# Moving modulation sums, their folds, one weight load and the mask copies inside a two-block transformer kernel

## The chip, the cores and the metric

The kernel runs on one core of one Trainium2 chip. The metric is the device time of one execution in microseconds (us), as the median of several runs.

## The reference

The input is one sequence of 512 tokens by 1024 channels in fp32, held transposed as 8 tiles of 128 x 512. The first block is the one that the change touches:

```
mod = silu(c) @ ada_w + ada_b             # six vectors of 1024
h = rms_norm(x, g) * (1 + sc_m) + sh_m
proj = h @ w_in                           # 3 mixers and gates
o_a, o_b, o_c = diff_attention, hgrn2 (scan), gla (scan)
merged = g_a*(o_a@w_up_a) + g_b*(o_b@w_up_b) + g_c*(o_c@w_up_c)
x = x + gt_m * (merged @ w_out)           # stage "out"
h = rms_norm(x, g2) * (1 + sc_f) + sh_f
x = x + gt_f * (square(relu(h @ mlp_w1)) @ mlp_w2)
```

The scans of b and c are gated linear recurrences in chunks. A second block follows (windowed attention, two gated convolution networks, a chunked spatial gating unit); the change does not touch it.

## The kernel before

Each fp32 product is made on TensorE in three matmuls: high part by high part, low by high, high by low. A weight unit of up to 128 x 2048 is loaded by SyncE's DMA queue into one of two buffers RAW. ScalarE copies it to WH (L1353) and GpSimd makes WL = RAW - WH (L2659), each in four quarters; `raw_free` is raised when GpSimd has finished, and the queue's next load into that buffer waits for it. SyncE's queue is in order: a load that waits holds back every load behind it.

**Modulation vectors.** The six vectors come from a product of a vector with a matrix. Only a part of it is made at the start. The rest ("shares") is made on VectorE: `shares(j, s)` is four instructions `acc = w * c[k] + acc` (128 x 512, L1917, the very first a plain product at L1914), s = 0 or 1 being the two halves of the 8 slabs. `fold(j)` on TensorE then sums the accumulator over the partitions by four one-column matmuls into a bank of PSUM, and `later_mod(j)` on VectorE adds the bias. Number 4 and 5 give the scale of the second norm, 6 and 7 the gate of the MLP. The matrix for j > 3 arrives by `load_later(a)` (L725) into two buffers LX; it waits until the shares have released the buffer, and sits in the same SyncE queue as the weight loads.

**Stage "out".** TensorE makes 4 tiles of unit ("out", 0), then 4 of ("out", 1), 12 matmuls of 512 columns each, into banks 3, 4, 5, 6 and 0, 1, 2, 3. VectorE empties each tile with one instruction that also adds the residual (X<-PS,MOD,X, L1917). Then `fold(4)` and `tail("out")` follow: units ("out", 2) and ("out", 3) in two halves of 256 columns, 8 output tiles each, with banks 0 to 3 in turn, so that tile k = 4 needs what `take(0, 0)` on VectorE empties. VectorE's order was

```
        shares(4, 0)
        shares(4, 1)
        for j in range(2):
            ... (four evictions of unit ("out", j))
            shares(5, j)
        later_mod(4)
        boundary("out")
```

**Boundary and MLP.** `boundary("out")` takes the tail's tiles, sums squares, scales by the second norm. The MLP is 16 units w1 and 16 units dn. TensorE runs w1 0 to 3, `fold(6)`, w1 4, dn 0, dn 1, `fold(7)`, dn 2, ... . VectorE's `mlp_in(p, i2)` squares and splits what ScalarE's relu left of a w1 unit.

**Scans.** For each of three scans r and 8 levels k a list of steps is placed into the common order of all engines: `product` (TensorE, into banks 4 and 5), `collect` (VectorE copies those banks under a mask into SCT, L2237), `scale` and `differ` for later levels (VectorE, DD, L1911), and after k = 3 `turn` (transposes on TensorE into banks 4 and 5), after k = 4 `state` (48 or 24 small matmuls into bank 4) and `carry` (VectorE, ST). `turn` and `state` need the banks that `collect` empties.

Of the kernel before, what the change touches and what calls it, by code (L numbers as in the profile page):

```python
# [176 lines left out]
class Events:  # L177
# [18 lines left out]
    def at(self, event):  # L196
        if event is None or self.counting:
            return None, 0
        return self.value[event]
# [35 lines left out]
class Plan:  # L235
# [134 lines left out]
    def recurrences(self):  # L370

        yield [("lag", 0)]
        yield [("differ", 0, 0)]
        yield [("expo", 0, 0), ("differ", 0, 1)]
        yield [("scale", 0, 0), ("expo", 0, 1)]
        for g, (r, k) in enumerate(LEVELS):
            for j in range(PAIRS[r]):  # L380
                last = j + 1 == PAIRS[r]
                one, two, three = [("product", r, k, j)], [], []
                if (r, k) == (2, 0):
                    two.append(("read", 1, 0))
                if j == 0 and g + 1 < len(LEVELS):
                    two.append(("scale", *LEVELS[g + 1]))
                if last and g + 2 < len(LEVELS) and LEVELS[g + 2][1] < 7:
                    two.append(("differ", *LEVELS[g + 2]))
                    three.append(("expo", *LEVELS[g + 2]))
                if last and k == 2:  # L390
                    two.append(("ends", r))
                    three.append(("reach_k", r))
                elif last and k == 3:
                    three.append(("turn", r))
                elif last and k == 4:
                    one.append(("eq", r))
                    three.append(("state", r))
                    three.append(("carry", r))
                elif last and k == 5:
                    two.append(("reach_q", r))  # L400
                    if r < 2:
                        three.append(("lag", r + 1))
                elif last and (r, k) == (0, 7):
                    one.append(("read", 0, 0))
                two.insert(0 if last and k in (3, 4) else len(two), ("collect", r, k, j))
                for at_, step in {(1, 0): ((one, 0), (three, 1), (three, 2)), (1, 1): ((one, 3),), (1, 2): ((one, 4), (three, 5), (three, 6)),
                                  (1, 3): ((two, 7),), (2, 0): ((three, 8),), (2, 1): ((three, 9), (three, 10)),
                                  (2, 2): ((two, 11),)}.get((r, k), ()):
                    at_.append(("norm", *(("c", 0), ("c", 1), ("b", 0))[step // 4], step % 4))
                if (r, k) == (1, 1):  # L410
                    three.append(("read", 0, 1))
                yield one
                yield two
                yield three
        yield [("read", 2, 0)]
        for n in range(4):
            yield [("norm", "b", 1, n)]
# [15 lines left out]
def build(nc, wts, xt, vec, mixc, masks, distw, wst, bsr, out, spill):  # L433
# [3 lines left out]
    up, at = ev.up, ev.at  # L437
# [15 lines left out]
    AF = place("AF", o, [8]); o += 32  # L453
# [186 lines left out]
    last_square = {1: 6, 2: 5}  # L640


    FOLDED = [3] * 4 + [7, 4, 7, 7]
    SHARES = [SQ] * 5 + [R, SQ, R]

    def early(*what):
# [8 lines left out]
    def sync_program(q):  # L655
# [73 lines left out]
        while done < len(units) - 9:  # L729
            done += 1  # L730
            load(done)
            for a, (tag, n) in ((10, ("out", 2)), (11, ("out", 3)), (12, ("w1", 0)), (13, ("w1", 0)), (14, ("w1", 3)), (15, ("w1", 4))):
                if done == U[tag, n]:
                    load_later(a)
        for hf in range(2):
# [7 lines left out]
    def tensor_program(q):  # L743
# [108 lines left out]
        def tail(name, u, xs, xk):  # L852

            for hf in range(2):
                four = name == "attn" and hf == 0
                for k in range(4) if four else ():
                    rows_half(BANK["tail", name, k, hf], hf, u[0], 128 * k, range(3), xs, xk, True, False, alone=True)
                for k in range(8):
                    i = u[k // 4]
                    b = BANK["tail", name, k, hf]  # L860
                    if four and k < 4:
                        t = rows_half(b, hf, i, 128 * k, [3], xs[3:], xk[3:], False, True)
                    else:
                        t = rows_half(b, hf, i, 128 * (k % 4), range(4), xs, xk, alone=True)
                    if k % 2:
                        t.then_inc(*up("psum", ("tail", name, k // 2, hf), *([("w", i)] if hf and k % 4 == 3 else [])))
                    elif (name, k, hf) == ("f1", 6, 1):
                        t.then_inc(*up("psum", ("tail_six",)))
                    holds(b, ("y_tail", name, k // 2, hf))
                    if (name, hf, k) == ("out", 0, 5):  # L870
                        fold(5)
                    if hf and k == 1:
                        sums_half(name, 0)

# [229 lines left out]
        def fold(j):  # L1104

            b = FOLDED[j]
            q.wait_ge(*at(("shares", j)))
            free(b)
            for m in range(4):
                t = mm(PS[:, b, m:m + 1], SHARES[j][:, 128 * m:128 * m + 128], ones[:, 0:1], True, True)  # L1110
            t.then_inc(*up("psum", ("folded", j)))
            holds(b, ("later_mod", j))
# [37 lines left out]
        for j in range(2):  # L1150
            tiles(U["out", j], mixed[0:4], [("merged", k) for k in range(4)], 3)
        fold(4)
        tail("out", [U["out", 2], U["out", 3]], mixed[4:8], [("merged", k) for k in range(4, 8)])
        w1 = [P.unit["mlp", "in", 0, n] for n in range(2)]
        head("out", "mlp", w1)
# [751 lines left out]
    def vector_program(q):  # L1907
# [40 lines left out]
        def boundary(n):  # L1948
# [19 lines left out]
            def scale(hf, k):  # L1968
                root = PS[:, ROOT[hf], 0:256]
                q.wait_ge(*at(("root", n, hf)))  # L1970
                if n == "out":
                    if k > 2:
                        q.wait_ge(*at(("h", "mlp", k - 3, hf)))
                    q.wait_ge(*at(("af",)))
                    t = stt(half(T0[1 + k % 3], hf), half(X[:, k, :], hf), gain["mlp"](k), root, MUL, MUL)
                    t.then_inc(*up("d_norm", ("sc", "mlp", k, hf), ("post", n, k, hf)))
                else:
                    if k > 1 or hf:
                        q.wait_ge(*at(("x_post", n, k - 2, hf) if k > 1 else ("x_post", n, 6 + k, 0)))
                    t = stt(half(PS[:, SUMS, :], k % 2), half(Y[:, k, :], hf), post[n](k), root, MUL, MUL)  # L1980
                    t.then_inc(*up("d_norm", ("post", n, k, hf)))
# [38 lines left out]
            for p in range(4):  # L2020
                take(0, p)
                if p > 1:
                    add(0, p - 1)
            if n == "out":
                later_mod(5)
                q.wait_ge(*at(("later_mod", 5)))
                stt(AF[:, :], MOD[:, 32:40], 1.0, v("gmlp", 0, 8), ADD, MUL).then_inc(*up("d_mix", ("af",)))
            add(0, 3)
            take(1, 0)
            if nx is None:  # L2030
# [279 lines left out]
        def later_mod(j):  # L2310
            q.wait_ge(*at(("folded", j)))
            tt(MOD[:, 16 + 4 * j:20 + 4 * j], PS[:, FOLDED[j], 0:4], v("ada_b", 16 + 4 * j, 4), ADD).then_inc(*up("d_ev", ("later_mod", j)))

# [65 lines left out]
        merged_low(7)  # L2379
        shares(4, 0)  # L2380
        shares(4, 1)
        for j in range(2):
            i = U["out", j]
            for m in range(4):
                k = 4 * j + m
                q.wait_ge(*at(("t", i, m)))
                q.wait_ge(*at(("x_again", k)))
                q.wait_ge(*at(("later_mod", 1)))
                stt(X[:, k, :], PS[:, BANK[i, m], :], MOD[:, 16 + k:17 + k], X[:, k, :], MUL, ADD).then_inc(*up("d_ev", ("ev", i, m)))
            shares(5, j)  # L2390
        later_mod(4)
        boundary("out")

        def stage(name, taken, given):
# [7 lines left out]
        def mlp_in(p, i2):  # L2402
            i = U["w1", 4 * p + i2]
            for m in range(2):
                n = 2 * i2 + m
                c = 8 * p + n
                q.wait_ge(*at(("ev", i, m)))
                if c > 1:
                    q.wait_ge(*at(("up_lo", (c - 2) // 8, (c - 2) % 8)))
                a_, b_ = TQ[n % 2][:, :], TQ[2 + n % 2][:, :]  # L2410
                tt(b_, a_, a_, MUL).then_inc(*up("d_mix", ("mlp_sq", c)))
                low(("up_hi", p, n), ("up_lo", p, n), UP[p % 2][:, n, 1, :], b_, UP[p % 2][:, n, 0, :])
            if (p, i2) == (0, 0):
                shares(6, 0)
                shares(6, 1)
            elif (p, i2) in ((0, 3), (1, 0)):
                shares(7, p)

        def mlp_out(p, j):
            i = U["dn", 4 * p + j]  # L2420
# [498 lines left out]
```

## Time and profile before

| | |
|---|---|
| runs shown | 2227.24, 2227.36, 2222.14 us |
| median | 2227.24 us |
| profiled execution, its own time | 2227.24 us |
| its span, first to last instruction | 2224.9 us |
| TensorE busy | 2187.4 us, 98% |
| VectorE, ScalarE, GpSimd busy | 50%, 39%, 48% |
| mean granted TensorE clock | 0.996 of full speed |

The span and the profiled execution's own time differ by 2.3 us, which lie around the span. An engine's busy time is the time in which it had an instruction of its own in work; idle time is listed with the instruction that ended it.

### The profile page before, as it was taken

What the parts mean: (1) busy time and instruction counts of PE and PEld (TensorE: products, weight loads), DVE (VectorE), ACT (ScalarE), POOL (GpSimd) and SP (SyncE); (2) the same over time, 40 slices, a digit from 0 to 9 for tenths busy, and PEclk for the clock granted to TensorE, in tenths of its full rate; (3) what the DMA queues carried; (4) which work ended last, traced back from release to release, by engine and by line L of the source; (5) the groups of instructions that cost most, each with busy time, mean ns of one, the idle gap of its engine ahead of it and who ended that gap; (6) DMA issues with size and microseconds to landing.
All of it is one profiled execution on the core that took longest, in us unless ns stands there. A gap on an engine that the chain in (4) does not pass through costs nothing.

```text
span 2224.9 us, 28773 instructions
## 1 busy us (share of the span) xinstructions
PE 2187.4 (98%) x11670; PEld 1823.6 (82%) x11670; DVE 1103.1 (50%) x1694; ACT 874.5 (39%) x1662; POOL 1068.9 (48%) x812
## 2 busy tenths in 40 slices
PE   7999999999999999999999999999999999999998
PEld 4788777878888888888888888888888889888887
DVE  4774657377622214485862434521634447625253
ACT  4554554353423324475432222543323235323234
POOL 2755554454454446534354454454444454544444
PEclk9999999999999999999999999999999999999999
DMA  7211224574223222212222232232222222222221
GB/s 310 76 60 67 74 86 166 188 290 171 114 97 112 92 98 95 97 58 77 76 95 95 84 109 103 84 114 95 95 95 76 95 95 77 95 100 90 103 105 58
DMA packets 41251, 237.27 MB, mean 107 GB/s; under 512 B 4640, under 2 KB 6816, under 8 KB 15776
## 3 DMA queue, kind: packets, MB, share of 16 engines
q1 hardware_dynamic: 39760, 232.67, 29.3%
q10 hardware_dynamic: 1360, 2.78, 0.4%
q8 instruction: 92, 1.51, 0.3%
q14 instruction: 39, 0.32, 0.0%
HBM read 225.99 MB, written 8.39 MB: 105 GB/s over the span
## 4 chain that ended last, share of the span: by engine, by line
PE 87%; DVE 7%; ACT 2%; issue 1%; DMA 1%; POOL 1%; SPq 0%; DVEq 0%; POOLq 0%; ACTq 0%
PE PS L755 86%; DMA RAW<-in_wts 1%; POOL WL L2659 1%; DVE HLO L1917 1%; PE PS L1202 1%; DVE PS L1917 1%; DVE X L1911 1%; DVE DD L1911 1%; DVE SQ L1917 0%; DVE VV L1914 0%; DVE SCT L2237 0%; DVE R L1917 0%; DVE X L1917 0%; DVE ZB L1911 0%; PE PS L1084 0%
## 5 line engine op out<-in xcount | busy, mean ns | idle before, releaser
L2659 POOL TENSOR_TENSOR WL<-RAW,WH 128x512 fp32r<-128x512 f32 (+1 forms) x688 | 917.8, 1363 | 1015.9 <-ACT WH L1353 990.1
L755 PE MATMUL PS<-HHI,WH 128*128 128x512 f32 x1488 | 594.6, 400 | 1.7 <-DVE HLO L1917 1.2
L755 PE MATMUL PS<-HHI,WL 128*128 128x512 f32 x1488 | 580.6, 390 | 0.0
L755 PE MATMUL PS<-HLO,WH 128*128 128x512 f32 x1488 | 580.4, 390 | 0.0
L1353 ACT ACTIVATE WH<-RAW 128x512 fp32r<-128x512 f32 (+1 forms) x688 | 378.6, 613 | 419.2 <-PE PS L755 380.2
L755 PEld LDWEIGHTS PS<-HHI,WH 128*128 128x128 f32 x1488 | 279.9, 188 | 74.6 <-issue 10.7
L755 PEld LDWEIGHTS PS<-HHI,WL 128*128 128x128 f32 x1488 | 279.8, 188 | 59.6
L755 PEld LDWEIGHTS PS<-HLO,WH 128*128 128x128 f32 x1488 | 280.2, 188 | 57.3 <-issue 2.4
L755 PE MATMUL PS<-UF,WH 128*128 128x512 f32 (+1 forms) x832 | 223.8, 357 | 0.0
L1911 DVE TENSOR_TENSOR T<-PS,R 128x512 f32<-128x512 f32 x112 | 76.9, 690 | 213.9 <-PE PS L755 208.5
L755 PEld LDWEIGHTS PS<-UF,WH 128*128 128x128 f32 x832 | 148.3, 189 | 22.7
L755 PE MATMUL PS<-UP,WH 128*128 128x512 f32 x512 | 157.7, 389 | 0.0
L1911 DVE TENSOR_TENSOR Y<-PS,Y 128x512 f32<-128x512 f32 (+1 forms) x97 | 66.3, 686 | 174.6 <-PE PS L755 174.6
L755 PE MATMUL PS<-UF,WL 128*128 128x512 f32 (+1 forms) x416 | 148.3, 356 | 0.0
L755 PEld LDWEIGHTS PS<-UP,WH 128*128 128x128 f32 x512 | 96.0, 188 | 19.8
L755 PE MATMUL PS<-WH,HHI 128*128 128x256 f32 (+1 forms) x320 | 110.3, 345 | 0.3 <-POOL WL L2659 0.3
L1855 ACT ACTIVATE TG<-TG 128x512 f32<-128x512 f32 x44 | 27.8, 632 | 206.5 <-DVE TG L1917 206.5
L755 PE MATMUL PS<-WH,HLO 128*128 128x256 f32 (+1 forms) x320 | 108.1, 338 | 0.0
L755 PE MATMUL PS<-WL,HHI 128*128 128x256 f32 (+1 forms) x320 | 108.1, 338 | 0.0
L1917 DVE SCALAR_TENSOR_TENSOR TG<-T,V,TG 128x511 f32<-128x511 f32 x88 | 104.5, 1188 | 3.1
L755 PE MATMUL PS<-UP,WL 128*128 128x512 f32 x256 | 99.6, 389 | 0.0
L755 PE MATMUL PS<-US,WH 128*128 128x512 f32 x320 | 99.0, 390 | 0.0
(345 smaller groups left out, 3206.5 us busy)
## 6 DMA issues: line engine op xcount, KB each, us to landing
RAW<-in_wts SPq DMA_DIRECT2D x182, 1024.0 KB, 4.8
LX<-in_wts SPq DMA_DIRECT2D x8, 1024.0 KB, 4.9
FW<-in_wts SPq DMA_DIRECT2D x6, 1024.0 KB, 12.3
spill<-T SPq DMA_DIRECT2D x24, 256.0 KB, 4.0
RAW<-in_wts SPq DMA_DIRECT2D x8, 768.0 KB, 4.1
GT<-spill SPq DMA_DIRECT2D x20, 256.0 KB, 5.1
X<-in_xt SPq DMA_DIRECT2D x2, 1024.0 KB, 6.8
out_x<-X SPq DMA_DIRECT2D x8, 256.0 KB, 2.3
```

The lines of the kernel that those rows point to most:

```text
L755: return e.matmul(o_, l, r, start=start, stop=stop)
L1202: t = e.transpose(PS[:, 2 + part, 128 * s:128 * s + 128], S[:, s, 128 * part:128 * part + 128], ident)
L1353: e.activation(WH[i][:, cs], RAW[i % 2][:, cs], ACT.Copy).then_inc(*up("w_hi", ("w_hi", i, p)))
L1855: e.activation(G, G, ACT.Gelu_apprx_tanh).then_inc(*up("a_ev", ("gelu", name, j)))
L1911: return e.tensor_tensor(o_, a, b, f)
L1917: return e.scalar_tensor_tensor(out=o_, in0=a, scalar=s, in1=b, op0=f1, op1=f2)
L2659: return e.tensor_tensor(o_, a, b, f)
```

## The change

1. In the scans `collect` of level 3 and 4 (the last pair) is no longer put ahead of `scale` and `differ`, but behind them, as for the other levels.
2. `shares(5, 0)` and `shares(5, 1)` are put ahead of the evictions of ("out", 0) and of ("out", 1), instead of behind them; `fold(5)` goes from inside the tail (after tile 5 of the first half) to the place ahead of it, and into bank 6 instead of 4; `later_mod(5)` and the gain AF = (1 + mod) * g go ahead of `boundary("out")`, out of its middle.
3. `shares(6, 1)` goes from behind `mlp_in(0, 0)` to behind `mlp_in(0, 1)`.
4. `load_later(13)` goes from behind the load of ("w1", 0) to behind that of ("w1", 1).

```diff
-                two.insert(0 if last and k in (3, 4) else len(two), ("collect", r, k, j))
+                two.append(("collect", r, k, j))
...
-    FOLDED = [3] * 4 + [7, 4, 7, 7]
+    FOLDED = [3] * 4 + [7, 6, 7, 7]
...
-... (12, ("w1", 0)), (13, ("w1", 0)), ...
+... (12, ("w1", 0)), (13, ("w1", 1)), ...
...
-                    if (name, hf, k) == ("out", 0, 5):
-                        fold(5)
...
         fold(4)
+        fold(5)
         tail("out", [U["out", 2], U["out", 3]], mixed[4:8], [("merged", k) for k in range(4, 8)])
...
-            if n == "out":
-                later_mod(5)
-                q.wait_ge(*at(("later_mod", 5)))
-                stt(AF[:, :], MOD[:, 32:40], 1.0, v("gmlp", 0, 8), ADD, MUL).then_inc(*up("d_mix", ("af",)))
...
         shares(4, 1)
+        shares(5, 0)
         for j in range(2):
             i = U["out", j]
+            if j == 1:
+                shares(5, 1)
             for m in range(4):
...
-            shares(5, j)
         later_mod(4)
+        later_mod(5)
+        q.wait_ge(*at(("later_mod", 5)))
+        stt(AF[:, :], MOD[:, 32:40], 1.0, v("gmlp", 0, 8), ADD, MUL).then_inc(*up("d_mix", ("af",)))
+        q.wait_ge(*at(("af",)))
         boundary("out")
...
-            if (p, i2) == (0, 0):
-                shares(6, 0)
-                shares(6, 1)
-            elif (p, i2) in ((0, 3), (1, 0)):
-                shares(7, p)
+            if (p, i2) in ((0, 0), (0, 1), (0, 3), (1, 0)):
+                shares(6 + (p or i2 == 3), 1 if p else i2 % 3)
```

## Rows read from the trace of the kernel before

**Rows 1.** The page: busy time, share of the span and instructions of each engine.

```profile
PE 2187.4 (98%) x11670; PEld 1823.6 (82%) x11670; DVE 1103.1 (50%) x1694; ACT 874.5 (39%) x1662; POOL 1068.9 (48%) x812
```

**Rows 2.** TensorE's waits: total us, times, longest.

```profile
PE PS L755 <- DVE X L1917: 2.0, 1, 2.0
```

**Rows 3.** Timeline of TensorE, stage "out": start, us, instruction, [idle before it].

```profile
513.55 0.39 PE L755 MATMUL PS<-ME,WL 128*128 128x512 f32 x1
514.45 0.95 PE L755 MATMUL PS<-V,SQ 128*128 128x1 f32 x8
...
523.27 0.50 PE L755 MATMUL PS<-ME,WH 128*128 128x256 f32 x2 [2.01 <-DVE X L1917]
```

**Rows 4.** Window behind that stop: length, busy time of each engine, granted clock, DMA.

```profile
523.00:528.00 5.00, 4.72 (x28) 4.73 (x28) 1.06 (x4) 3.23 (x6) 3.52 (x3) 0.66 0.91 341
```

**Rows 5.** Timeline of VectorE, stage "out" (x: instructions merged into the row).

```profile
508.02 2.71 DVE L1917 SCALAR_TENSOR_TENSOR X<-PS,MOD,X 128x512 f32<-128x512 f32 x4
510.65 0.47 DVE L1914 TENSOR_SCALAR R<-LX,CC 128x512 f32<-128x512 f32 x1
511.16 2.33 DVE L1917 SCALAR_TENSOR_TENSOR R<-LX,CC,R 128x512 f32<-128x512 f32 x3
...
516.04 6.33 DVE L1917 SCALAR_TENSOR_TENSOR R<-LX,CC,R 128x512 f32<-128x512 f32 x4
...
522.36 1.65 DVE L1917 SCALAR_TENSOR_TENSOR X<-PS,MOD,X 128x256 f32<-128x256 f32 x4
```

**Rows 6.** Timeline of GpSimd in the same stage.

```profile
504.54 5.96 POOL L2659 TENSOR_TENSOR WL<-RAW,WH 128x512 fp32r<-128x512 f32 x4 [2.22 <-ACT WH L1353]
515.42 6.39 POOL L2659 TENSOR_TENSOR WL<-RAW,WH 128x512 fp32r<-128x512 f32 x4 [4.91 <-PE PS L755]
```

**Rows 7.** Timeline of SyncE's queue, `load_later(12)` and `load_later(13)`.

```profile
513.52 9.20 SPq L725 DMA_DIRECT2D LX<-in_wts  x2
```

**Rows 8.** Timeline of all engines at the start of the MLP.

```profile
573.24 5.55 DVE L1917 SCALAR_TENSOR_TENSOR SQ<-LX,CC,SQ 128x512 f32<-128x512 f32 x7
575.97 0.43 SPq L665 DMA_DIRECT2D RAW<-in_wts  x1
...
579.19 10.77 SPq L665 DMA_DIRECT2D RAW<-in_wts  x2
582.96 2.20 ACT L1353 ACTIVATE WH<-RAW 128x512 fp32r<-128x512 f32 x4 [10.88 <-DMA RAW<-in_wts]
...
590.71 0.95 PE L755 MATMUL PS<-V,SQ 128*128 128x1 f32 x8
590.85 0.69 DVE L1911 TENSOR_TENSOR UP<-TQ,UP 128x512 fp32r<-128x512 f32 x1 [0.70 <-ACT UP L1758]
```

**Rows 9.** Timeline of all engines, first scan, level 4.

```profile
132.78 1.34 DVE L2237 COPY_PREDICATED SCT<-MASK,PS 128x1024 f32<-128x1024 uint8 x1
134.02 1.80 DVE L1911 TENSOR_TENSOR DD<-Am 128x512 f32<-128x512 f32 x1
134.73 0.88 PE L755 MATMUL PS<-VC,KN 128*32 128x64 f32 x48
135.74 0.28 DVE L2257 COPY ST<-PS 128x128 f32<-128x128 f32 x1
...
137.09 1.19 PE L755 MATMUL PS<-DD 32*128 32x128 f32 x16 [1.48 <-DVE ST L1917]
```

**Rows 10.** Timeline of all engines, third scan, level 3, and TensorE's next wait.

```profile
331.81 1.31 DVE L2237 COPY_PREDICATED SCT<-MASK,PS 128x1024 f32<-128x1024 uint8 x1
333.02 2.12 DVE L1911 TENSOR_TENSOR DD<-QKB,DD 128x512 f32<-128x512 f32 x2
335.06 1.77 DVE L1911 TENSOR_TENSOR DD<-Am 128x512 f32<-128x512 f32 x1
335.75 0.81 PE L1032 MATMUL PS<-V,KH 128*128 128x128 f32 x6
...
347.47 0.50 PE L755 MATMUL PS<-HHI,WH 128*128 128x512 f32 x1 [0.58 <-ACT T L1701]
```

More of the change, by code:

```diff
@@ L731, in sync_program @@
             load(done)
-            for a, (tag, n) in ((10, ("out", 2)), (11, ("out", 3)), (12, ("w1", 0)), (13, ("w1", 0)), (14, ("w1", 3)), (15, ("w1", 4))):
+            for a, (tag, n) in ((10, ("out", 2)), (11, ("out", 3)), (12, ("w1", 0)), (13, ("w1", 1)), (14, ("w1", 3)), (15, ("w1", 4))):
                 if done == U[tag, n]:
@@ L1973, in scale @@
                         q.wait_ge(*at(("h", "mlp", k - 3, hf)))
-                    q.wait_ge(*at(("af",)))
                     t = stt(half(T0[1 + k % 3], hf), half(X[:, k, :], hf), gain["mlp"](k), root, MUL, MUL)
```

## The prediction

> **What bounds the kernel now.** The page comes first: TensorE is busy for 98% of the span, every other engine for at most half of it [rows 1]. So only what stops TensorE, or lowers its clock, costs time, and an edit can win no more than the stops it removes. The list of TensorE's waits comes second: one of 2.0 us on an eviction X of VectorE [rows 2] lies in stage "out", where most of the change lies. Third, the timeline of TensorE there: the fold of shares 4 starts at 514.45, the tail follows, and its tile k = 4 stands still for 2.01 us before 523.27 [rows 3]. Fourth, the granted clock just behind: 0.66 over 5 us [rows 4], a mix of the full 2.4 GHz and of 1.2 GHz. Against full clock that costs 5 x (1 - 0.66) = 1.7 us; below I call this a slow spell. Fifth, VectorE's timeline, which has no gap from 508.02 to the take at 522.36 [rows 5]: the eight shares 5 stand between the evictions and the take that TensorE waits for.
>
> Two prices are read off there. A share costs 2.33 / 3 = 0.78 us when GpSimd is idle and 6.33 / 4 = 1.58 us when GpSimd works [rows 5, 6]; an eviction costs 2.71 / 4 = 0.68 us. Matmuls of 512 columns start every (514.45 - 513.55) / 4 = 0.225 us [rows 3].
>
> **Part 2, stage "out".** The edit removes no work from VectorE; it changes what TensorE meets first.
> - `shares(5, 0)` now starts at 508.02, in place of the first eviction. GpSimd works until 504.54 + 5.96 = 510.50 [rows 6], so two of its four instructions cost 1.58 and two 0.78: it ends at 508.02 + 4.72 = 512.7. The first eviction then ends at 513.4.
> - Who is queued behind: tile 3 of ("out", 1) uses the bank which that eviction frees. It is due 12 matmuls ahead of the fold, at 514.45 - 12 x 0.225 = 511.75. TensorE stops for 1.65 us; ("out", 1) ends at 516.1, `fold(4)` (about 0.9 us) at 517.0.
> - The four evictions end at 512.7 + 2.7 = 515.4. `shares(5, 1)` follows. GpSimd's next pieces start 0.97 us behind the end of ("out", 1) (514.45 to 515.42 [rows 3, 6]), so at 517.1: two shares at 0.78, two at 1.58, end at 520.1.
> - `fold(5)` now stands ahead of the tail and waits for that: TensorE stops from 517.0 to 520.1, 3.1 us. The tail starts behind it.
> - The old stop of 2.01 goes: the take has nothing ahead of it any more. The fold itself is moved, not added. `later_mod(5)` and AF are two tiny instructions and lie beside the tail's first tiles; without that cover they would cost some 0.3 us.
> Stops: 1.65 + 3.1 - 2.01 = +2.7 us. I count one slow spell before and one after. Bounds: all eight shares at 0.78 give 1.25 us of stop and no spell, -0.8 - 1.7 = -2.5; all at 1.58 give stops of 3.3 and 4.75, +6.0, and with a second spell +7.7. I take +2.7, since GpSimd's pieces cover about half of the eight.
>
> **Part 3, `shares(6, 1)`.** Now eight shares 6 run from 572.7 to 578.8 without a gap [rows 8], long ahead of `fold(6)` at 590.71 on TensorE. In the changed kernel the last four wait for `mlp_in(0, 1)`. That step is not early: ScalarE's relu stands behind its conversion of ("w1", 4), which waits for a load issued at 575.97 until 582.96, and VectorE's last instruction of the step ends at about 591.5 [rows 8]. Nothing in the change moves this load: it stands behind `load_later(14)`, which waits for `shares(6, 0)`. Four shares at 0.78 (GpSimd has nothing to do there) end at 591.5 + 3.1 = 594.6. TensorE, in order, stands at `fold(6)` from 590.71 to 594.6: +3.9 us, with ("w1", 4) and all of the rest queued behind. A stop twice as long as the one of rows 3 should bring a slow spell as that one did: +1.7. Sum +5.6. Bounds: 3.9 without a spell; 7.1 with all four at 1.58, 8.8 with a spell.
>
> The Trainium skill ("TensorE: Matmul & The Clock Gate", Part 1: The HAM clock gate) has only these two clocks and ties the low one to idleness and the high one to sustained work. Read strictly, a stop in which `fold(6)` and matmuls stand on both sides need not lower the clock; the sum would then be 1.7 us less. The trace speaks for the spell: 2.01 us of stop were enough [rows 3, 4].
>
> What is late next: `load_later(15)` waits for these shares and holds back the loads behind it, which now go out from 579.19 on [rows 8], to about 595. The first, ("dn", 0), takes some 7 us behind another one (575.97 to 582.96) and lands at 602; its first quarter is ready at about 604. TensorE comes to it at 594.6 + 0.9 + 48 x 0.227 = 606.4. So nothing, with 2 us to spare; if the cover is gone, a stop of 1 to 3 us and perhaps a spell.
>
> **Part 1, `collect` last.** It wins nothing where TensorE does not wait for `scale` or `differ`, and it never does in the list of waits. It costs where TensorE comes to `turn` or `state` early.
> - First scan, level 4: today `collect` 132.78 to 134.02, `differ` 1.80 us beside `state` (134.73, 0.88 us), then `carry` from 135.74, and TensorE goes on at 137.09 [rows 9]. In the new order: `differ` to 134.6, `collect` to 135.8, `state` to 136.7, `carry` 1.35 us to 138.05: +1.0 us. Bounds: 0 (`differ` at an uncontended price) and 1.8.
> - Third scan, level 3: `turn` runs at 335.75 [rows 10]. In the new order `scale` (2.04) and `differ` (1.77) come first, `collect` ends at 331.81 + 3.8 + 1.2 = 336.8: +1.1. At 347.47 TensorE waits 0.58 us for ScalarE, which hangs on a load and not on TensorE; that wait is used up. Net +0.5, bounds 0 and 1.3.
> - At the other places TensorE comes later than all three instructions in either order: 0.
>
> **Part 4, `load_later(13)`.** Today SyncE stands 9.2 us between the two issues [rows 7] and the load of ("w1", 1) behind it; in the new order that load waits for GpSimd's last pieces alone. TensorE waits for neither: 0. If the cover were gone, the later of the two waits would count, 1 to 2 us.
>
> **Sum**, against the profiled execution's own time, 2227.24 (which is also the median): 2227.2 + 1.0 + 0.5 + 2.7 + 5.6 = 2237.0 us.
>
> **Rivals.**
> - A, forecast: stops at tile 3, `fold(5)`, `fold(6)`, and a spell behind the last. 2237, own range 2234.5 to 2240. Chance 0.53.
> - B, the clock stays high behind `fold(6)`, or the first scan and "out" cost only half of what I count: 2227.2 + 1.5 + 2.7 + 3.9 = 2235.3, or down to 2232. For it: the spells are few, 0.996 over the span. Against it: rows 4. Chance 0.22.
> - C, knock-on: ("dn", 0) arrives too late, or "out" has a spell behind each of its two stops. +2 to +4 on A: 2240. For it: 15 us of delay in the weight queue. Against it: 2 us to spare. Chance 0.15.
> - D, not slower: the stop at `fold(6)` does not exist. One mechanism: the conversion of ("w1", 4) gets its load so early that `mlp_in(0, 1)` ends by 590.71 - 3.1 = 587.6, 3.9 us ahead of rows 8; the point is a landing at 579 instead of 583. With the stage "out" at its lower bound the time is 2227.2 + 1.5 - 2.5 = 2226.2. For it: the queue is freed of its 9.2 us stand. Against it: this load is tied to `shares(6, 0)`, not to that stand. Chance 0.10; with it a real gain, which would need nearly all stops of the kernel to go.
>
> **How the numbers follow.** About 0.3% (6.7 us, so 2233.9) is what a measurement of this kernel can tell from no change. Slower by more: nearly all of A and C and a third of B, 0.74. Within: 0.23. Faster: the far end of D, 0.03. The range that should hold 8 in 10 runs from the low part of B to the high part of C: 2231 to 2241.5.
>
> **What would show it.** In TensorE's waits of the changed kernel: one of about 3.9 us at `fold(6)` on a VectorE instruction that writes SQ; one of about 3 us at `fold(5)` on R; one of 1 to 2 us on the first eviction; none on the take; about 2.5 us in all on ST and SCT in the first scan; a low clock behind `fold(6)`. The prediction is wrong if the eight shares 5 end before TensorE has finished ("out", 1), or if `mlp_in(0, 1)` is over long before 591.

## The result, and the profile after

The changed kernel took 2240.73 us (median of 4 runs, 2240.13 to 2245.01), the kernel before 2226.21 us beside it (4 runs, 2222.14 to 2227.36): ratio 1.0073, 95% interval 1.0054 to 1.0091. In a second set of runs it was 2241.94 against 2225.0 us, ratio 1.0077 (1.0062 to 1.0092). The forecast was 2237.0, or +9.8 us; measured are +14.5 and, by the ratios, +16 to +17. The sign held and the sum was too small by some 5 us (by the ratios some 7). The median lies in the stated range, 2231 to 2241.5, but near its upper end: the second set's 2241.94 lies just beyond it, and so does 2243.5, which is the ratio times the 2227.24 that the forecast started from.

The profiled execution has an own time of 2242.2 us. Its line of busy times answers to [rows 1]:

```profile
PE 2192.2 (98%) x11670; PEld 1826.9 (82%) x11670; DVE 1109.5 (50%) x1694; ACT 874.9 (39%) x1662; POOL 1071.9 (48%) x812
```

Nothing shows there: the work is the same, and 15 us are 0.7% of the span. TensorE's waits tell more (us in total, times, longest us):

```profile
PE PS L755 <- DVE SCT L2231: 6.7, 4, 2.5
PE PS L755 <- DVE SQ L1916: 3.8, 1, 3.8
...
PE PS L1030 <- DVE SCT L2231: 2.2, 1, 2.2
PE PS L755 <- DVE R L1916: 2.1, 1, 2.1
PE PS L755 <- DVE X L1916: 1.6, 1, 1.6
PE PS L755 <- DVE ST L1916: 1.4, 1, 1.4
...
PE PS L755 <- DVE T L1910: 1.1, 3, 0.8
```

Against [rows 2], SQ at `fold(6)`, SCT at `turn` (L1030) and R at `fold(5)` are new; the wait on X is now for the first eviction, and the one of 2.0 us on the take is gone. SCT at L755 was 3.2 us in 2 waits before, and is now 6.7 in 4.

The same matmul's start can be compared in the two traces. The difference grows in steps: +1.1 at 134.8 us (`state`, first scan), +4.0 from 336.9 (`turn`, third scan), +3.2 from 348.5 (`state`, third scan), +1.9 over stage "out", +6.7 from 590.3 (`fold(6)`), +1.1 at 1592. That is 18.0; 0.75 is given back at 459. What is left down to 15.5 at the end lies ahead of 142 us and is not of the change: the changed kernel's trace is 2.6 us late by 53 us (1.0 in its first 20 us, 1.6 by low clock), and the other loses 3.0 and 1.5 us to low clock from 107 to 114 and from 138 to 142 us.

The granted clock in the stretches behind those stops (stretch, length, busy times, PEclk, DMA share, GB/s), as in [rows 4]:

```profile
336.00:342.00 6.00, 4.74 (x22) 4.10 (x22) 1.75 (x2) 3.25 (x7) 0.00 (x0) 0.72 0.49 179
353.50:358.50 5.00, 4.21 (x35) 3.64 (x36) 3.27 (x8) 1.26 (x3) 0.65 (x1) 0.70 0.37 102
519.50:525.00 5.50, 3.61 (x20) 3.03 (x19) 5.39 (x7) 2.56 (x5) 1.87 (x2) 1.00 0.69 282
526.00:530.00 4.00, 4.00 (x23) 4.00 (x23) 2.73 (x6) 0.00 (x0) 2.75 (x3) 0.57 0.12 18
601.00:606.00 5.00, 3.66 (x13) 3.28 (x14) 3.57 (x6) 2.21 (x4) 0.00 (x0) 0.52 0.55 175
606.00:610.00 4.00, 4.00 (x15) 3.18 (x14) 2.61 (x5) 1.77 (x4) 0.00 (x0) 0.74 1.01 418
```

Length times (1 - clock) gives what each would cost with TensorE at work throughout: 1.7, 1.5 (1.7 with the 3.5 us that follow, at 0.94), 0, 1.7, and 2.4 + 1.0 = 3.4 us at `fold(6)`. Of the last not all was lost, because the low clock began while TensorE still stood: the fold starts at 602.34, and the window from 601 has the clock at 0.52. The matmuls there fall back by 6.7 us, the stop is 3.8, so 2.9 us were the clock's. In PE's rows a 512-column matmul then takes 0.63 us instead of 0.39.

**Stage "out"** (timeline of all engines; it answers to [rows 3, 5, 6]):

```profile
513.81 1.51 DVE L1913 TENSOR_SCALAR R<-LX,CC 128x512 f32<-128x512 f32 x1
515.36 3.24 DVE L1916 SCALAR_TENSOR_TENSOR R<-LX,CC,R 128x512 f32<-128x512 f32 x3
518.51 2.72 DVE L1916 SCALAR_TENSOR_TENSOR X<-PS,MOD,X 128x512 f32<-128x512 f32 x4
519.31 0.73 PE L755 MATMUL PS<-ME,WH 128*128 128x512 f32 x2 [1.62 <-DVE X L1916]
521.14 3.99 DVE L1916 SCALAR_TENSOR_TENSOR R<-LX,CC,R 128x512 f32<-128x512 f32 x4
523.13 5.61 POOL L2656 TENSOR_TENSOR WL<-RAW,WH 128x512 fp32r<-128x512 f32 x4 [6.66 <-PE PS L755]
525.19 1.05 PE L755 MATMUL PS<-V,R 128*128 128x1 f32 x8 [2.08 <-DVE R L1916]
```

Tile 3 waits 1.62 us for the first eviction, `fold(5)` 2.08 us for the last share. Four shares took 3.99 us, three at 0.75 and one at 1.64 us, the one that began behind the start of GpSimd's pieces at 523.13.

**`fold(6)`** (the same view; it answers to [rows 8]):

```profile
590.67 2.20 ACT L1352 ACTIVATE WH<-RAW 128x512 fp32r<-128x512 f32 x4 [10.89 <-DMA RAW<-in_wts]
...
598.57 0.69 DVE L1910 TENSOR_TENSOR UP<-TQ,UP 128x512 fp32r<-128x512 f32 x1 [0.70 <-ACT UP L1757]
599.18 3.11 DVE L1916 SCALAR_TENSOR_TENSOR SQ<-LX,CC,SQ 128x512 f32<-128x512 f32 x4
602.34 1.87 PE L755 MATMUL PS<-V,SQ 128*128 128x1 f32 x8 [3.77 <-DVE SQ L1916]
```

It is the chain that was forecast: a conversion that waited for its load, relu, the last instruction of `mlp_in(0, 1)`, four shares of 3.11 us, the fold.

**Third scan** (the same view, levels 3 and 4; it answers to [rows 10]):

```profile
329.05 3.17 POOL L2656 TENSOR_TENSOR WL<-RAW,WH 128x512 fp32r<-128x512 f32 x2
331.00 3.21 DVE L1910 TENSOR_TENSOR DD<-QKB,DD 128x512 f32<-128x512 f32 x2
332.18 1.49 POOL L2656 TENSOR_TENSOR DD<-Am 128x512 f32<-128x512 f32 x1
334.14 1.77 DVE L1910 TENSOR_TENSOR DD<-Am 128x512 f32<-128x512 f32 x1
335.83 1.29 DVE L2231 COPY_PREDICATED SCT<-MASK,PS 128x1024 f32<-128x1024 uint8 x1
337.26 0.85 PE L1030 MATMUL PS<-V,KH 128*128 128x128 f32 x6 [2.19 <-DVE SCT L2231]
...
346.32 3.02 POOL L2656 TENSOR_TENSOR WL<-RAW,WH 128x512 fp32r<-128x512 f32 x2 [10.97 <-ACT WH L1352]
348.11 3.22 DVE L1910 TENSOR_TENSOR DD<-QKB,DD 128x512 f32<-128x512 f32 x2
...
352.93 1.30 DVE L2231 COPY_PREDICATED SCT<-MASK,PS 128x1024 f32<-128x1024 uint8 x1
354.29 0.92 PE L755 MATMUL PS<-VB,KN 128*64 128x64 f32 x24 [2.47 <-DVE SCT L2231]
```

GpSimd in the same stretch of the kernel before:

```profile
329.87 3.18 POOL L2659 TENSOR_TENSOR WL<-RAW,WH 128x512 fp32r<-128x512 f32 x2
333.01 1.58 POOL L2659 TENSOR_TENSOR DD<-Am 128x512 f32<-128x512 f32 x1
334.55 1.73 POOL L2659 TENSOR_TENSOR WL<-RAW,WH 128x512 fp32r<-128x512 f32 x1
```

`scale`, the two DD<-QKB, took 3.21 us; before, behind `collect`, it took 2.12 [rows 10]. GpSimd works without a gap in either order, until 336.28 and 335.36. `collect` takes 1.3 us in either place: beside GpSimd it loses nothing. The halves of `scale`, read one by one, take 1.77 and 1.52 us in the new order, 0.67 and 1.53 in the old one. There the first half began at 333.02, within 0.01 us of the start of a new piece of GpSimd; in the new order it began at 331.00, 0.5 us into a piece, and was the longer by 1.1 us. So the same three instructions take 1.1 us longer in the new order, and `turn` is late by 2.2 us and not by 1.1. In each of the seven traces with level 3 of the third scan late the halves take 1.77 and 1.52 us, give or take 0.01; in nine of the ten others they take 0.67 and 1.53.

### The profile page after: what moved, and what is told of

Its sections match the earlier page's. It is cut to its first block and busy times, and to the rows that moved or that the text cites. A ratio compares the mean times of both kernels' runs of the same rounds, so it can differ in the third digit from the quotient of the medians.

```text
span 2240.4 us, 28770 instructions
## 1 busy us (share of the span) xinstructions
PE 2192.2 (98%) x11670; PEld 1826.9 (82%) x11670; DVE 1109.5 (50%) x1694; ACT 874.9 (39%) x1662; POOL 1071.9 (48%) x812
## 5 line engine op out<-in xcount | busy, mean ns | idle before, releaser
L755 PE MATMUL PS<-HHI,WH 128*128 128x512 f32 x1488 | 594.6, 400 | 1.2 <-DVE HLO L1916 1.2
L755 PE MATMUL PS<-HHI,WL 128*128 128x512 f32 x1488 | 581.5, 391 | 0.0
L755 PE MATMUL PS<-HLO,WH 128*128 128x512 f32 x1488 | 581.1, 391 | 0.0
L755 PEld LDWEIGHTS PS<-HHI,WH 128*128 128x128 f32 x1488 | 280.3, 188 | 73.8 <-issue 10.5
L755 PEld LDWEIGHTS PS<-HHI,WL 128*128 128x128 f32 x1488 | 280.2, 188 | 59.3
L755 PEld LDWEIGHTS PS<-HLO,WH 128*128 128x128 f32 x1488 | 280.4, 188 | 57.3 <-issue 2.4
L755 PE MATMUL PS<-UF,WH 128*128 128x512 f32 (+1 forms) x832 | 223.9, 357 | 0.0
L755 PEld LDWEIGHTS PS<-UF,WH 128*128 128x128 f32 x832 | 148.3, 189 | 22.7
L755 PE MATMUL PS<-UP,WH 128*128 128x512 f32 x512 | 157.8, 389 | 0.0
L755 PE MATMUL PS<-UF,WL 128*128 128x512 f32 (+1 forms) x416 | 148.3, 356 | 0.0
L755 PEld LDWEIGHTS PS<-UP,WH 128*128 128x128 f32 x512 | 96.1, 188 | 20.0
L755 PE MATMUL PS<-WH,HHI 128*128 128x256 f32 (+1 forms) x320 | 110.3, 345 | 0.3 <-POOL WL L2656 0.3
L755 PE MATMUL PS<-WH,HLO 128*128 128x256 f32 (+1 forms) x320 | 108.2, 338 | 0.0
L755 PE MATMUL PS<-WL,HHI 128*128 128x256 f32 (+1 forms) x320 | 108.1, 338 | 0.0
L755 PE MATMUL PS<-US,WH 128*128 128x512 f32 x320 | 99.2, 391 | 0.8 <-DVE T L1910 0.8
L755 PE MATMUL PS<-UP,WL 128*128 128x512 f32 x256 | 99.6, 389 | 0.0
```

The source lines that it names most:

```text
L755: return e.matmul(o_, l, r, start=start, stop=stop)
```

## The experiments

Unless said otherwise each is the kernel before with the edit shown. A median is of 5 to 11 executions, and the ratio is to the kernel before, run beside it on the same chip; 0.1% is 2.2 us.

| kernel | median us | ratio | 95% interval |
|---|---|---|---|
| part 1 alone | 2232.67 | 1.0032 | 1.0020 to 1.0044 |
| part 1 alone, again | 2231.56 | 1.0031 | 1.0020 to 1.0043 |
| part 2 alone | 2226.56 | 1.0004 | 0.9995 to 1.0012 |
| part 3 alone | 2231.19 | 1.0027 | 1.0018 to 1.0036 |
| part 4 alone | 2226.28 | 1.0002 | 0.9993 to 1.0011 |
| changed, part 1 undone | 2234.06 | 1.0049 | 1.0034 to 1.0063 |
| changed, part 3 undone | 2235.70 | 1.0050 | 1.0037 to 1.0063 |
| part 1, level 3 only | 2226.61 | 1.0006 | 0.9997 to 1.0014 |
| part 1, level 4 only | 2225.53 | 1.0004 | 0.9995 to 1.0013 |
| part 1, first scan only | 2226.58 | 1.0013 | 1.0003 to 1.0023 |
| part 1, third scan only | 2227.14 | 1.0015 | 1.0003 to 1.0026 |
| `collect` of level 2 first too | 2226.00 | 1.0007 | 0.9998 to 1.0015 |
| shares 5 between the takes | 2220.18 | 0.9979 | 0.9970 to 0.9987 |

### Each part alone

```diff
-                two.insert(0 if last and k in (3, 4) else len(two), ("collect", r, k, j))
+                two.append(("collect", r, k, j))
```

> Part 1 alone: collect of levels 3 and 4 behind scale and differ, all else as before. Theory S (the order of VectorE costs two stops in the third scan, at turn and at state, besides the small one in the first scan): 4 to 8 us slower than before, and the third scan shows one TensorE wait of about 2 us on SCT at turn (L1030 or so) and one of about 2.5 us at state. Theory P (the prediction's: +1.0 in the first scan, +0.5 in the third; the rest of what was seen is the clock's chance): 1 to 2 us slower, with at most one wait of 1 us in the third scan.

Part 2 alone is all of the change's point 2, of which these are the main lines:

```diff
+        shares(5, 0)
         for j in range(2):
+            if j == 1:
+                shares(5, 1)
...
-            shares(5, j)
...
-                    if (name, hf, k) == ("out", 0, 5):
-                        fold(5)
...
+        fold(5)
         tail("out", [U["out", 2], U["out", 3]], mixed[4:8], [("merged", k) for k in range(4, 8)])
...
```

> Part 2 alone: shares 5 ahead of the evictions, fold(5) ahead of the tail. Theory S (two stops of 1.6 and 2.1 us take the place of the one of 2.0): +1.7 us of stops, one slow spell as before, 1 to 3 us slower. Rival (the stage is worth nothing alone, or even wins because the take is no longer late): 0 to 3.7 us faster.

Part 3 alone:

```diff
-            if (p, i2) == (0, 0):
-                shares(6, 0)
-                shares(6, 1)
...
+            if (p, i2) in ((0, 0), (0, 1), (0, 3), (1, 0)):
+                shares(6 + (p or i2 == 3), 1 if p else i2 % 3)
```

> Part 3 alone: shares(6, 1) behind mlp_in(0, 1). Theory S: TensorE stops for 3.8 to 3.9 us at fold(6) and the clock is low for 3.4 to 6.8 us behind it: 5.5 to 7.3 us slower. Rival (the stop is a consequence of the other parts shifting the loads): no stop at fold(6), within 1 us of before.

Part 4 alone:

```diff
-... (13, ("w1", 0)), ...
+... (13, ("w1", 1)), ...
```

> Part 4 alone: load_later(13) one load later. Both theories: within 0.5 us of before; the load of (w1, 1) goes out at 521.8 instead of 522.8. Rival: if the order of the queue matters here, a shift of more than 1 us at the head of the MLP.

**Measured.** By their ratios: part 1 +7.1 us (4.5 to 9.8), part 2 +0.9 (-1.1 to 2.7), part 3 +6.0 (4.0 to 8.0), part 4 +0.4 (-1.6 to 2.4). They sum to 14.4 us, against 16.3 us (12.0 to 20.3) for the whole change. Part 2 alone has its two stops (R 2.1, X 1.6 us) in place of the one of 2.0, as in the changed kernel. Part 3 alone has the stop and one low stretch of the length that was forecast (timeline of TensorE; windows):

```profile
593.00 1.05 PE L755 MATMUL PS<-V,SQ 128*128 128x1 f32 x8 [3.81 <-DVE SQ L1917]
```

```profile
593.00:598.00 5.00, 5.00 (x19) 4.13 (x20) 3.13 (x5) 2.67 (x5) 0.00 (x0) 0.66 0.77 295
```

So 3.8 + 5 x 0.34 = 5.5 us. Part 1 is the surprise. Its waits of TensorE:

```profile
PE PS L755 <- DVE SCT L2237: 4.2, 3, 2.5
...
PE PS L1032 <- DVE SCT L2237: 2.1, 1, 2.1
```

`turn` waits 2.1 us here too, and one SCT wait of 1.0 is new, at `state` of the first scan. The clock behind that `state`, in the kernel before:

```profile
137.00:141.00 4.00, 3.91 (x29) 3.75 (x30) 4.00 (x6) 1.95 (x3) 0.00 (x0) 0.64 0.61 233
141.00:145.00 4.00, 4.00 (x33) 4.00 (x33) 3.15 (x3) 2.12 (x5) 1.40 (x1) 0.94 0.03 6
```

and with part 1 alone:

```profile
137.00:141.00 4.00, 2.80 (x19) 2.58 (x20) 3.93 (x9) 1.99 (x3) 0.00 (x0) 0.65 0.62 242
141.00:145.00 4.00, 4.00 (x21) 4.00 (x20) 3.97 (x4) 0.00 (x0) 0.00 (x0) 0.50 0.00 0
```

1.7 us were lost to the clock there, now 3.4: the stop of 1.1 us is followed by a low stretch twice as long. That is a matter of how often, and not of always: of the seven traces in which level 4 of the first scan is late, five have the long stretch (6.8 us) and the two of the changed kernel have none; of the other ten, three have one of 3.4 us and seven none. On average that is 2.4 us against 0.5, an estimate from 17 traces.

### The changed kernel with one part undone, and part 1 again

> The changed kernel with part 1 undone (collect of levels 3 and 4 first again). If the parts add, as their single runs say (part 1 about 7 us, part 2 about 1, part 3 about 5 to 6, part 4 nothing): 6 to 7 us slower than before, no wait at turn. If part 1 was costly only by itself and not beside the others: 12 to 14 us slower.

> The changed kernel with part 3 undone (shares(6, 1) behind mlp_in(0, 0) again). If the parts add: 7 to 9 us slower than before, and no wait at fold(6). Rival (the stop at fold(6) is due to the late load that part 4 or part 2 moved): the wait stays, 12 us slower or more.

> Part 1 alone once more. Level 3 alone and level 4 alone came out at 1.0006 and 1.0004, both together at 1.0032. Theory S2 (the third scan's stop at turn is 2.1 us in every execution, and what follows depends on whether the clock falls behind it: then TensorE and VectorE are late enough to make a further stop at state): this run gives 3 to 7 us slower again, a turn wait of 2.1 us, and a state wait only if a low clock lies between. Rival (the two levels add to 2 us and the first run was chance): 1 to 3 us slower.

> The kernel before once more, one look: which waits and slow spells come back. Every theory: the same waits (2.5 and 0.8 us on SCT, 1.5 on ST, 2.0 on X) within 0.1 us. Where the clock is low ahead of and behind them may differ; if the spells of the first scan (6.8 and 3.4 us) are missing, they are no property of the kernel.

**Measured.** Without part 1 the change costs 10.9 us, without part 3 11.1 us, whole 16.3: each of the two is worth some 5 us in the company of the others as well, with an uncertainty of some 4 us. Both came out above the 6 to 7 and 7 to 9 us that the single runs had led to expect; the profile without part 1 loses 3.4 us to the clock behind `fold(6)` (0.57 over 593 to 601 us), where part 3 alone lost 1.7. Part 1 alone gave 1.0031 after 1.0032, so its price is no accident of one set of runs. The stops that the change makes come back in every trace to 0.1 us (`turn` 2.1 or 2.2, R 2.0 or 2.1, X 1.6, SQ 3.8 or 3.9). The low stretches do not: the kernel before, profiled a second time (own time 2221.84 us), shows the first line, where its first profile has the second:

```profile
107.00:114.00 7.00, 6.70 (x51) 5.46 (x52) 4.22 (x7) 6.68 (x12) 6.26 (x5) 1.00 0.10 37
```

```profile
107.00:114.00 7.00, 6.38 (x26) 5.25 (x27) 4.43 (x6) 6.51 (x12) 5.93 (x5) 0.53 0.13 56
```

### Part 1 split by level

```diff
-                two.insert(0 if last and k in (3, 4) else len(two), ("collect", r, k, j))
+                two.insert(0 if last and k == 4 else len(two), ("collect", r, k, j))
```

> collect behind scale and differ for level 3 only (level 4 stays ahead of them). If the cost of part 1 lies at turn of the third scan (2.1 us of wait on SCT, often with a slow spell behind it): 2 to 4 us slower than before, that wait present, no wait at the third state and 1.5 us on ST in the first scan as before. If it lies at state: same as before, no wait at turn.

The other half has `k == 3` in that place.

> collect behind scale and differ for level 4 only. If the cost lies at the states: the first scan has a wait of 1.1 us on SCT ahead of state besides 1.4 us on ST, and the third scan's state waits for 1 to 2.5 us: 2 to 4 us slower. If the third state waits only because turn made TensorE and VectorE late before it: no wait there, 1 us slower, all in the first scan.

**Measured.** Level 3 late, expected to cost 2 to 4 us, cost 1.3 (-0.7 to 3.1). It has the wait of 2.2 us at `turn` and no growth of SCT at L755 (3.2 us); level 4 late has SCT 4.2 us and no wait at `turn`. So the stops belong where they were put. The times do not add up as well: 1.0006 and 1.0004 against 1.0032 for both. At the upper ends of their intervals the two would reach 1.0027.

### Part 1 split by scan, and the changed kernel again

```diff
-                two.insert(0 if last and k in (3, 4) else len(two), ("collect", r, k, j))
+                two.insert(0 if last and k in (3, 4) and r > 0 else len(two), ("collect", r, k, j))
```

> The kernel before with collect late (levels 3 and 4) in the first scan only. Theory: ST's and SCT's stops at state of the first scan grow by 1.1 us, no other wait is new, and the low-clock stretch behind them is as long or up to twice as long: 1.1 to 2.8 us slower, ratio 1.0005 to 1.0013. Rival (the unexplained half lies in the first scan, since its stop lengthens the slow spell in every execution): ratio 1.002. The wait of 0.8 us near 1592 us should be absent in both.

The third scan alone has `r < 2` in that place.

> The kernel before with collect late in the third scan only (the second scan stays as before too). Theory: one new wait of 2.2 us at turn, the DVE wait of 0.8 us near 1592 us if it comes from this scan's delay, and a slow spell behind the turn in part of the executions: 2.2 to 4.5 us slower, ratio 1.001 to 1.002. Rival (the halves do not add because the state of the third scan is also late once both levels are late): a wait of 1.5 to 2.5 us on SCT at state near 350 us as well, ratio 1.002 to 1.003.

The changed kernel a second time, 4 executions:

> The changed kernel a second time. The stops (turn 2.2, tile 3 of stage out 1.6, fold(5) 2.1, fold(6) 3.8 us) return with the same lengths to 0.1 us; the low-clock stretches behind them may change place or length; ratio 1.006 to 1.008. Theory: the stop of 2.5 us at state of the third scan is no property of the part alone, since no kernel with part 1 alone shows it; it returns only if the clock falls behind the turn again. Rival: it belongs to the changed kernel and is there whatever the clock does.

**Measured.** Split this way the ratios add, as far as their intervals tell: 1.0013 and 1.0015, 6.2 us of the 7.1. The first scan costs 2.9 us (0.7 to 5.1), the third 3.3 us (0.7 to 5.8). Their profiles show the stops (SCT 4.3 us at L755 in the one, 2.2 us at L1032 in the other). The wait of 0.8 us near 1592 us came in the profile of the first scan's kernel, where it was expected not to.

The changed kernel's second trace agrees with its first to 0.3 us at every matmul, low stretches and the wait of 2.5 us at `state` of the third scan included. Whether that wait needs the low clock behind `turn` can be read beside the kernel with the third scan alone, whose `turn` is just as late but whose clock stays high (timeline of TensorE, windows, timeline of VectorE):

```profile
338.10 0.85 PE L1032 MATMUL PS<-V,KH 128*128 128x128 f32 x6 [2.19 <-DVE SCT L2237]
```

```profile
336.00:341.50 5.50, 3.40 (x22) 3.01 (x24) 2.58 (x3) 3.31 (x7) 0.19 (x1) 1.00 0.32 91
```

```profile
346.58 1.29 DVE L1911 TENSOR_TENSOR DD<-QKB,DD 128x512 f32<-128x512 f32 x2
347.79 1.79 DVE L1911 TENSOR_TENSOR DD<-Am 128x512 f32<-128x512 f32 x1
349.50 1.33 DVE L2237 COPY_PREDICATED SCT<-MASK,PS 128x1024 f32<-128x1024 uint8 x1
```

From the start of `turn`, `scale` starts 8.5 us later here, 10.9 us later in the changed kernel. Here it is nearly done when GpSimd's pieces begin (347.42) and takes 1.29 us; there it meets them and takes 3.22, and `collect` behind it ends too late for `state`. Of the six traces with both levels of the third scan late, the four whose clock stays high behind `turn` lack the second wait, and the two of the changed kernel, with the low clock, have it. That fits the theory (the wait is a follower of the clock), but the clock was not varied by itself, so it is a reading and not a proof.

### Two versions meant to win

First, `collect` of level 2 put first as well, since TensorE waits 2.5 us on an SCT in the kernel before too:

```diff
-                two.insert(0 if last and k in (3, 4) else len(two), ("collect", r, k, j))
+                two.insert(0 if last and k in (2, 3, 4) else len(two), ("collect", r, k, j))
```

> Before, with collect of level 2 put first as well. In the first scan TensorE waits 2.5 us for that collect, which stands behind differ (1.46) and ends (0.16). Theory S: that wait falls to about 1 us: 1 to 3 us faster. Rival: VectorE is the bound of the first scan as a whole and the wait comes back at the next product: within 0.5 us of before.

```profile
PE PS L755 <- DVE SCT L2237: 2.0, 3, 1.0
PE PS L755 <- ACT KN L1632: 1.5, 1, 1.5
```

The wait fell from 2.5 to 1.0 us, and ScalarE, which needs what `differ` writes, is now late by 1.5 us: 1.0007 (0.9998 to 1.0015), nothing won.

Second, the stop of [rows 2] taken away at its root: in the kernel before, `shares(5, 1)` no longer stands as a block ahead of the take, but is cut up between the takes, and `fold(5)` goes behind tile 7:

```diff
-                    if (name, hf, k) == ("out", 0, 5):
+                    if (name, hf, k) == ("out", 0, 7):
...
-            shares(5, j)
+            if j == 0:
+                shares(5, 0)
...
             for p in range(4):
+                if n == "out":
+                    for kk in ((0, 1), (2,), (3,), ())[p]:
+                        ada(5, 1, kk)
                 take(0, p)
```

> Before, with shares(5, 1) cut up between the takes of the tail (two instructions, take 0, one, take 1, one, take 2) and fold(5) behind tile 7 instead of 5. Theory S says the 2.0 us stop at tile 4 of the tail is the take standing behind four shares at 1.6 us; then it goes, with the slow spell behind it: 2 to 3.7 us faster. If the stop were set by the sum of VectorE's work and not by its order, it returns at tile 6 or at the fold: within 1 us of before.

```profile
513.55 2.87 DVE L1917 SCALAR_TENSOR_TENSOR R<-LX,CC,R 128x512 f32<-128x512 f32 x2
516.34 0.86 DVE L1917 SCALAR_TENSOR_TENSOR X<-PS,MOD,X 128x256 f32<-128x256 f32 x2
517.13 1.01 DVE L1917 SCALAR_TENSOR_TENSOR R<-LX,CC,R 128x512 f32<-128x512 f32 x1
518.76 0.88 DVE L1917 SCALAR_TENSOR_TENSOR X<-PS,MOD,X 128x256 f32<-128x256 f32 x2 [0.63 <-PE PS L755]
```

```profile
522.00:528.00 6.00, 6.00 (x53) 6.00 (x52) 3.50 (x9) 1.20 (x2) 2.76 (x3) 1.00 0.96 375
```

TensorE has no wait on X any more, and the clock of 522 to 528 is 1.00, where it was low behind the stop [rows 4]. The ratio is 0.9979 (0.9970 to 0.9987), 4.7 us won (2.9 to 6.7) where stop and low clock together were worth 3.7. It is the fastest kernel of this study.

## Why the prediction was right or wrong

| step, in us | forecast | trace of the changed kernel | by the runs, alone |
|---|---|---|---|
| first scan | +1.0 | +1.1 stop; clock varies | +2.9 |
| third scan | +0.5 | 4.0 + 3.2 - 0.75 = +6.5 | +3.3 |
| near 1592 us | 0 | +1.1 | within the first scan's |
| stage "out" | +2.7 | +1.9 | +0.9 |
| `shares(6, 1)` | +5.6 | +6.7 | +6.0 |
| load | 0 | 0 | +0.4 |

- **The step that failed is Part 1, third scan: "Net +0.5, bounds 0 and 1.3".** The place and the mechanism were right (`turn` needs the banks that `collect` empties), the size was not. `scale` was entered at 2.04 us, its duration behind `collect`. But a duration from a row holds for its neighbours: moved ahead, its first half took 1.77 us instead of 0.67, the price of an instruction beside GpSimd, and the whole 3.21. The two prices of the prediction's own first part, 0.78 and 1.58 us, say so, and were not used here; none of the prediction's rows for this stretch is of GpSimd, which works through all of it. The stop was 2.19 us instead of 1.1; less the 0.58 us used up at 347.47, as forecast, that is 1.6, outside the bounds.
- The same part put two more terms at nothing. The low clock: one was added behind `fold(6)`, none in Part 1, and the stop at `turn` brought one of 1.7 us in both profiles of the changed kernel. "At the other places [...] 0": in the changed kernel TensorE also waited 2.5 us at `state` of the third scan, with another 1.7 us of low clock. The first scan's stop was right to 0.1 us (+1.0, measured +1.1). Alone that scan costs about 2.9 us (0.7 to 5.1, so 1.0 is not excluded); its trace shows the low stretch behind the stop twice as long and the wait near 1592 us.
- **Part 2.** Both stops came where they were put: 1.62 us (forecast 1.65) at tile 3, and at `fold(5)` 2.08 us (forecast 3.1). The second was forecast too long mainly because one share, not two, ran beside GpSimd. One low stretch before, one behind `fold(5)` now: as counted, though the take's stop had one behind it in only 6 of the 11 traces that have that stop.
- **Part 3.** The stop was 3.77 us (forecast 3.9), by the chain that was named. The low clock cost 1.7 us with part 3 alone, as forecast, and 2.9 us in the changed kernel. It came with `fold(6)` in each of the four traces that have the stop. The Trainium skill ("TensorE: Matmul & The Clock Gate", Part 1: The HAM clock gate) ties the low clock to idleness, and in the prediction's strict reading a stop with matmuls on both sides need not lower it: at `fold(6)` it did each time, at `turn` (2.2 us) in two traces of seven. ("dn", 0) came in time, as forecast: no wait on it is in the list.
- **Part 4** is worth nothing, as forecast.
- **Rivals.** The stops are those of A. The time is C's 2240, but by luck and not for C's reasons: its late ("dn", 0) and its second low stretch in "out" did not occur; part 1 made up the difference. B fell with the clock behind `fold(6)`, D with the stop there.
- **Open.** Why the levels add to 0.1% and the scans to 0.28% of the 0.32% (the intervals leave room for chance). Why a wait of 0.8 us near 1592 us, where VectorE's T<-T,T takes 1.65 us, comes with each of the seven traces in which level 3 of the first scan is late, over a thousand us earlier, and with no other. What decides whether a given stop is followed by a low stretch. And why the first half of `scale` was quick beside GpSimd at 333.02 us and none that began in the midst of a piece was stays open too: no run varies the start.

## What to carry to other kernels

Before an instruction is moved on one engine, read what the other engines do in the stretch it is moved into: its duration is that of its place, and an instruction that bears company well (here `collect`, 1.3 us in either place) may be the right one to leave there. On an engine that waits strictly in order, work that nobody needs soon, such as the shares, belongs in small pieces behind what the busy engine waits for next, and a fold behind work that can run meanwhile. Price each stop of TensorE with the low clock that may follow it: in this kernel stops of 1.6 to 3.8 us carried another 0 to 3.4 us.

## What was not expected of the hardware

- The stops that the change makes or removes come back to 0.1 us in every execution that was profiled, the low stretches do not: the kernel before had a clock of 0.53 over 107 to 114 us once and 1.00 the other time, and its two profiles end 4.9 us apart. Yet the changed kernel's two traces agree within 0.3 us, low stretches included.
- The length of a stop does not settle what follows it. Over all profiles, low clock came with the stop of 1.6 us at tile 3 in none of five (1.00 over 519.5 to 525 us in the changed kernel), with the one of 2.0 us on the take in six of eleven, with the one of 2.1 us at `fold(5)` in five of five (0.57 over 526 to 530), with the one of 2.2 us at `turn` in two of seven (0.72 in the changed kernel, 1.00 with the third scan alone), and with the one of 3.8 us at `fold(6)` in four of four, where it cost 1.7 us (part 3 alone), 2.9 (changed kernel) or 3.4 (without part 1).
- Beside GpSimd VectorE's work on SBUF operands slows by a factor of two or more (`scale` 1.29 to 3.22 us for two instructions, a share 0.78 to 1.58). `collect`, which reads PSUM under a mask, stays at 1.3 us, and four evictions, which read PSUM too, took 2.71 us while GpSimd worked [rows 5, 6] and 2.72 while it stood (518.51).
